# Expert weights of a two-block model read as halves of full rows, in eight rotating slots

## The reference

```python
D_MODEL, SEQ, N_EXPERTS, CAPACITY_FACTOR = 1024, 256, 16, 2
def expert_choice_moe(h, w_router, w_gate, w_up, w_down):
    cap = max(1, CAPACITY_FACTOR * S // N_EXPERTS)          # 32 tokens for each expert
    logits = jnp.einsum('bsd,de->bse', h, w_router).astype(jnp.float32)
    aff = jax.nn.softmax(logits, axis=-1)
    gate, idx = lax.top_k(aff.transpose(0, 2, 1), cap)
    xin = jax.vmap(lambda hb, ib: hb[ib])(h, idx)
    hid = jax.nn.silu(jnp.einsum('becd,edf->becf', xin, w_gate)) * jnp.einsum('becd,edf->becf', xin, w_up)
    y = jnp.einsum('becf,efd->becd', hid, w_down) * gate[..., None].astype(h.dtype)
    return jnp.zeros_like(h).at[bidx, idx].add(y)
...
x = x + einsum(mixed, w_out)                                 # end of the first block's mixer
x = x + expert_choice_moe(rms_norm(x, norm2_w[l]), ...)      # 16 experts
x = second_block(x, ...)                                     # 2 x (FFN, mixer, FFN)
```

## Time and profile before

| | |
|---|---|
| time, median of 3 runs | 1729.85 us (1727.73 to 1731.01) |
| span of the profiled execution, first to last instruction | 1726.3 us |
| time of the profiled execution itself | not listed apart from the three runs; its span lies 3.55 us under their median |
| PE busy | 1606.1 us, 93% of the span |
| DVE, ACT busy | 43%, 38% |
| read from HBM | 398.23 MB |
| mean granted TensorE clock | 0.936 of full speed |

### The profile page before, as it was taken

How to read it: one execution, slowest core, us unless ns; L and a number is a source line. 1 busy time by engine, 2 the same in 40 slices (tenths; PEclk the granted TensorE clock), 3 DMA queues, 4 the chain that set the end, 5 groups by cost and what they waited for, 6 DMA issues and landing times.

```text
span 1726.3 us, 26493 instructions
## 1 busy us (share of the span) xinstructions
PE 1606.1 (93%) x10974; PEld 1299.6 (75%) x10974; DVE 750.1 (43%) x1004; ACT 663.7 (38%) x757; POOL 46.6 (3%) x34
## 2 busy tenths in 40 slices
PE   7996878897888888999999999999999999999998
PEld 7885744443443444499999979999999999889997
DVE  4679531110101101164445765444554447754444
ACT  5564322111111111354345554433634354753343
POOL 0015200000000000000000000000000000000000
PEclk9898979788778878999999999999999999999999
DMA  7522599999999999965555535555465555346552
GB/s 241 178 80 73 198 339 386 387 387 387 387 387 387 387 387 387 369 220 179 185 191 158 163 98 196 193 178 163 152 215 191 174 170 182 115 138 202 193 181 86
DMA packets 249052, 400.12 MB, mean 232 GB/s; under 512 B 4720, under 2 KB 135200, under 8 KB 248864
## 3 DMA queue, kind: packets, MB, share of 16 engines
q1 hardware_dynamic: 247808, 397.74, 66.8%
q10 hardware_dynamic: 1184, 1.57, 0.3%
HBM read 398.23 MB, written 1.06 MB: 231 GB/s over the span
## 4 chain that ended last, share of the span: by engine, by line
PE 65%; SPq 20%; DVE 5%; DMA 4%; issue 3%; ACT 3%; POOL 0%; ACTq 0%; DVEq 0%; POOLq 0%
SPq L430 20%; PE ps L581 12%; PE ps L583 12%; PE ps L582 12%; PE ps L606 6%; PE ps L607 6%; PE ps L608 6%; PE ps L811 4%; DMA ring<-w_in 2%; PE ps L552 2%; PE ps L543 1%; PE ps L800 1%; DMA ring<-w_expert_down 1%; PE ps L844 1%; PE ps L854 1%
## 5 line engine op out<-in xcount | busy, mean ns | idle before, releaser
L1715 DVE TENSOR_TENSOR wl_sb<-raw_sb,wh_sb 128x2048 fp32r<-128x2048 f32 x162 | 370.8, 2292 | 294.1 <-ACT wh_sb L1220 293.8
L581 PE MATMUL ps<-xTh_sb,wh_sb 128*128 128x256 f32 x1696 | 482.2, 284 | 1.0 <-DVE xTl_sb L1410 1.0
L583 PE MATMUL ps<-xTh_sb,wl_sb 128*128 128x256 f32 x1696 | 479.9, 283 | 0.0
L582 PE MATMUL ps<-xTl_sb,wh_sb 128*128 128x256 f32 x1696 | 479.9, 283 | 0.0
L1220 ACT ACTIVATE wh_sb<-raw_sb 128x2048 fp32r<-128x2048 f32 x162 | 309.8, 1915 | 300.0 <-PE ps L583 186.4
L581 PEld LDWEIGHTS ps<-xTh_sb,wh_sb 128*128 128x128 f32 x1696 | 325.3, 192 | 4.5 <-DVE xTl_sb L1410 2.5
L582 PEld LDWEIGHTS ps<-xTl_sb,wh_sb 128*128 128x128 f32 x1696 | 325.4, 192 | 2.2 <-issue 0.7
L583 PEld LDWEIGHTS ps<-xTh_sb,wl_sb 128*128 128x128 f32 x1696 | 325.4, 192 | 0.0
L811 PE MATMUL ps<-ring,work 128*32 128x512 f32 x1280 | 206.0, 791 | 60.8 <-DMA ring<-w_expert_up 38.9
L811 PEld LDWEIGHTS ps<-ring,work 128*32 128x32 f32 x1280 | 45.7, 136 | 182.6 <-issue 153.1
L606 PE MATMUL ps<-wh_sb,hidh_sb 128*128 128x512 f32 x384 | 151.2, 394 | 1.2 <-DVE wl_sb L1715 1.2
(11 more groups left out here) (294 smaller groups left out, 1775.2 us busy)
## 6 DMA issues: line engine op xcount, KB each, us to landing
ring<-w_expert_down SPq DMA_DIRECT2D x32, 2048.0 KB, 19.7
ring<-w_expert_gate SPq DMA_DIRECT2D x24, 2048.0 KB, 19.4
ring<-w_expert_up SPq DMA_DIRECT2D x24, 2048.0 KB, 19.8
raw_sb<-ffn_gate SPq DMA_DIRECT2D x44, 1024.0 KB, 5.4
raw_sb<-ffn_up SPq DMA_DIRECT2D x44, 1024.0 KB, 5.3
raw_sb<-ffn_down SPq DMA_DIRECT2D x44, 1024.0 KB, 4.9
raw_sb<-w_in SPq DMA_DIRECT2D x22, 1024.0 KB, 5.4
ring<-w_in SPq DMA_DIRECT2D x16, 1024.0 KB, 5.6
```

Of the source, the lines that this page charges most:

```text
L581: pe.matmul(to, w_h[:, k, fs], x_h[:, k, :], start=k == 0, stop=False)
L582: pe.matmul(to, w_h[:, k, fs], x_l[:, k, :], start=False, stop=False)
L583: mm = pe.matmul(to, w_l[:, k, fs], x_h[:, k, :], start=False, stop=k == KD - 1)
L1715: dve.tensor_tensor(wl[j], raw[j], wh[j].bitcast(F32), ALU.subtract).then_inc(raw_free[j], 1)
```

## The change

Each matrix is again fetched in two DMAs of 2 MiB, but a half is now 512 of the 1024 rows with all 1024 columns: a run in HBM is one row, 4 KB, and partition p gets four rows. The 96 halves of the 16 experts are one sequence (gate 0, gate 1, up 0, up 1, down 0, down 1, next expert), half q goes to slot q % 8, and SP waits only for half q - 8 to have been used. As a half now holds part of the rows for all columns, a product writes two PSUM banks and needs both halves before either bank is complete: gate in banks 4 and 5, up in 6 and 7, down in 4 and 5 again. The gather of the next expert's tokens moves from the head of an expert to between the fold of gate and the fold of up, into bank 6. The transpose moves to the head of an expert. The silu is one instruction over all features instead of two. The first fetches of the second block, which go over slots 0 and 1, wait for expert 14 to be done; before, they waited for the last products of gate.

```diff
-            def half(row, w, c, to, landed):
-                rows = w.rearrange("e d f -> (e d) f")[bass.ds(row, D), 512 * c:512 * c + 512]
-                sp.dma_start(to, rows.rearrange("(k p) n -> p k n", p=P)).then_inc(landed, 16)
+            def half(i, row, s):
+                rows = (wg, wu, wd)[i // 2].rearrange("e d f -> (e d) f")[bass.ds(row, D), :]
+                lines = rows.rearrange("(k p) n -> p k n", p=P)
+                sp.dma_start(expert_rows(s), lines[:, (i % 2) * Q4:(i % 2 + 1) * Q4, :]).then_inc(ex_in[s], 16)
...
+            def next_half(q, taken, row):
+                sp.wait_ge(sem["half_used"], taken)
+                half(q % 6, row, q % NS)
+            TURN = 4 * 6
+            with sp.Fori(0, (NE * 6 - NS) // TURN) as g:
+                for j in range(TURN):
+                    next_half(NS + j, sp.snap(TURN * g + j + 1), sp.snap(4 * D * g + D * ((NS + j) // 6)))
+            for q in range(NS + (NE * 6 - NS) // TURN * TURN, NE * 6):
+                next_half(q, q - NS + 1, D * (q // 6))
...
+            def product(b, stationary, q, landed):
+                h, w = q % 2, expert_rows(q % NS)
+                pe.wait_ge(ex_in[q % NS], landed)
+                for n in range(2):
+                    for j in range(Q4):
+                        mm = pe.matmul(bank(b + n)[j * CAP:j * CAP + CAP, :], stationary[:, Q4 * h + j, :],
+                                       w[:, j, 512 * n:512 * n + 512], start=h == 0, stop=h == 1, skip_group_check=True)
+                    if h == 1 and n == 0:
+                        mm.then_inc(sem["n0_ps"], 1)
+                mm.then_inc(sem["half_used"], 1)
...
+                product(GATE_PS, xin, q, landed(q))
+                product(GATE_PS, xin, q + 1, landed(q + 1))
+                pe.wait_ge(sem["back_done"], e_th(1, 1))
+                product(UP_PS, xin, q + 2, landed(q + 2))
+                product(UP_PS, xin, q + 3, landed(q + 3))
+                pe.wait_ge(sem["g4_done"], e_th(2, 2))
+                fold_up(g4, GATE_PS, range(KD)).then_inc(sem["fold_ps"], 1)
+                pe.wait_ge(sem["hot_done"], e_th(1, 2))
+                pe.wait_ge(sem["u4_done"], e_th(2, 1))
                 gather()
+                pe.wait_ge(sem["u4_done"], e_th(2, 2))
+                fold_up(u4, GATE_PS + 1, range(Q4)).then_inc(sem["fold_ps"], 1)
+                fold_up(u4, UP_PS + 1, range(Q4, KD)).then_inc(sem["fold_ps"], 1)
+                pe.wait_ge(sem["ehid_done"], e_th(2, 1))
+                product(GATE_PS, hidT, q + 4, landed(q + 4))
+                pe.wait_ge(sem["ehid_done"], e_th(2, 2))
+                product(GATE_PS, hidT, q + 5, landed(q + 5))
+                pe.wait_ge(sem["y4_act"], e_th(1, 1))
+                pe.wait_ge(sem["y4_dve"], e_th(1, 1))
```

More of the change, by code:

```diff
@@ L259, in two_blocks @@
         r_mx, r_nm, r_sum, r_rec = t2(TT), t2(TT), t2(TT), t2(TT)
-        affT, topw, chosen, place, ones_e = [t2(S)[0:NE, :] for _ in range(5)]
+        topw, chosen, place, ones_e = [t2(S)[0:NE, :] for _ in range(4)]
         top8 = t2(8)[0:NE, :]
@@ L450, in _ @@
             sp.wait_ge(sem["w1_lo"], W1)
-            half(0, wu, 0, slot(2), ex_in[2])
+            half(2, 0, 2)
             sp.wait_ge(sem["acc_done"], 1)
-            for i, w, c in REST[1:]:
-                half(0, w, c, slot(i), ex_in[i])
-            first_half(D, True)
+            for i in range(3, 6):
+                half(i, 0, i)
+            for i in range(2):
+                half(i, D, 6 + i)
             sp.wait_ge(sem["tb_rows_done"], 1)
             sp.dma_start(tb_dram.ap(), tb_rows).then_inc(sem["tb_out"], 16)
[L459 to L482, removed]
@@ new lines, in fold_up, with expert, value, landed @@
+            def fold_up(src, b, ks):
+                for i, k in enumerate(ks):
+                    mm = pe.matmul(bank(b)[:, i * CAP:i * CAP + CAP], src[:, k, :], fold, start=True, stop=True)
+                return mm
+            def expert(g, i):
+                def value(per, v):
+                    return pe.snap(per * g + v)
+                def landed(q):
+                    return value(16 * TURN // NS, 16 * (q // NS) + 16)
+                def e_th(per, v):
+                    return value(4 * per, per * i + v)
+                q = 6 * i
+                pe.wait_ge(sem["hote_done"], e_th(1, 1))
+                for t in range(TT):
+                    mm = pe.transpose(bank(UP_PS + 1)[:, t * P:t * P + P], hot_e[:, t, :, :].rearrange("p j c -> p (j c)"), ident)
+                mm.then_inc(sem["back_ps"], 1)
+                pe.wait_ge(sem["xe_ready"], e_th(1, 1))
+                product(GATE_PS, xin, q, landed(q))
[7 more added lines that the diff above has]
+                pe.wait_ge(sem["u4_done"], e_th(2, 1))
+                gather()
+                pe.wait_ge(sem["u4_done"], e_th(2, 2))
[7 more added lines that the diff above has]
+                pe.wait_ge(sem["y4_dve"], e_th(1, 1))
+                for t in range(TT):
+                    for n in range(2):
@@ L856, in expert @@
                     mm.then_inc(sem["stage_done" if t else "half_done"], 1)
+            TURN = 4 * 6
             pe.wait_ge(sem["tb_rows_done"], 1)
-            with pe.Fori(0, NE // 2) as i:
-                expert(i, 0)
-                expert(i, 1)
+            pe.wait_ge(sem["hot_done"], 1)
+            gather()
+            with pe.Fori(0, NE // 4) as g:
+                for i in range(4):
+                    expert(g, i)
             def parts(j, n):
@@ L1957, in _ @@
             pool.memset(ones_e, 1.0).then_inc(sem["masks_zero"], 1)
-            pool.memset(hot[:, :, NE, :], 0.0).then_inc(sem["masks_zero"], 1)
-            pool.wait_ge(sem["used0"], 2 * NE)
+            pool.memset(hot[:, :, NE:NE + 2, :], 0.0).then_inc(sem["masks_zero"], 1)
+            pool.wait_ge(sem["half_used"], 6 * (NE - 1))
             for j in range(3):
                 pool.memset(hold[:, 1 + j:2 + j], 0.0).then_inc(raw_free[j], 1)
+            pool.wait_ge(sem["half_used"], 6 * (NE - 1) + 3)
+            for j in range(3):
+                pool.memset(hold[:, 6 + j:7 + j], 0.0).then_inc(used[j], 1)
             pool.wait_ge(sem["stage_done"], NE)
```

153 lines of the change are left out of this document (54 added, 99 removed).

## The result

The changed kernel takes 1709.92 us (median of 4 runs, 1707.82 to 1712.10) against 1730.43 us before (4 runs, 1727.73 to 1731.70): a ratio of 0.989 with an interval of 0.987 to 0.991. The forecast was 1708.8 us, 1.1 us less. The four runs fall into two pairs: 1707.8 and 1707.9 at a mean granted clock of 0.937 and 0.936, 1712.0 and 1712.1 at 0.925. The profiled execution is one of the slower pair (1711.96 us, 2.0 above the median). A run's time is about 1.8 us longer than its span, so the profiled execution of before, with a span of 1726.3, took about 1728.1 us, 2.3 under the median. So the two traces differ by 16.1 us where the medians differ by 20.5.

What follows compares the result with a forecast made beforehand. The prediction took the expert fetch stream at 387 GB/s to bound the first block. Stream -26.1, ahead +1, behind +4 gave -21.1 us, from 1729.85 to 1708.8 us; range from one below 1700 up to 1720.

Steps and rivals of the forecast that it cites:

- The rate of the stream: Expert fetches: 4 KB runs raise the long stream from 387 to 409 GB/s, so 88 halves take 26.1 us less.
- The line of 37.7 ns for a kilobyte and 9 ns for a run: Expert fetches: time per run from the rates at 1 and 2 KB, giving 160.1 ns or 409 GB/s at 4 KB.
- The 4.2 us kept for the slow start and the last landing: Stream's two ends: time left over when 88 halves are summed from SP's first reissue, kept the same before and after.
- Ahead of the stream: Before SP's first reissue: DVE's `hot_e` products and two transposes now come first, moving it to about 243.7; +1 us (0 to 2).
- Behind the stream: Last landing to end of last scatter: new fetch order leaves more PE work there; +4 us, 2.2 at full clock, +18 at low.
- The 0.7 us for DVE's multiply: After the last expert's fold of up: DVE's multiply with its wait, counted as 0.7 us ahead of down.
- The two signs that the forecast named for this place: End of the last expert: last scatter 8 to 14 us behind the last landing, and near 708 us.
- The cover: Inside the experts: PE keeps pace with the stream, 29.7 us an expert against a new period of 30.7, holding by 1.0 us.
- rival B: Inside the experts: PE becomes the bound, at a mean clock of about 0.79 instead of 0.82; 1722 us, chance 0.11.
- Edits at nothing: `xin` wait gone, `y4` wait added, one silu, SP's issues, second block's first fetches: all hidden or unchanged, no time.
- The sum: Whole kernel: -26.1 + 1 + 4 = -21.1 us, taking the median from 1729.85 to 1708.8 us.
- its bounds 401 GB/s and +9 us: Forecast's own limits: stream rate 401 to 413 GB/s, end +2 to +9 us, given as 1703 to 1718 us; chance 0.74.

Runs made afterwards that it cites:

- e1: The changed kernel with each half fetched as two 1 MiB DMAs cut by columns, so runs are 2 KB again; 1737.78 us, ratio 1.0040 to the kernel before.
- e2: The changed kernel with each half fetched as two 1 MiB DMAs cut by rows, so runs stay 4 KB; 1709.49 us, ratio 0.9873 to the kernel before.
- e4: The changed kernel fetching only half the rows, products using them twice, so PE's work is the same but output is wrong; 1683.65 us, ratio 0.9715.
- e3: The changed kernel with 16 KB runs, PE's left operands of gather and fold read with a step of four elements; 1759.09 us, ratio 1.0163.
- e6: The changed kernel with the scatter waiting for each copy of `y4` only where it reads it; 1712.08 us, ratio 0.9894.
- e10: The changed kernel with the gather moved between down's products and the scatter, and the last expert's gather left out; 1708.74 us, ratio 0.9874.
- e8: The changed kernel with 16 KB runs, feature order set in ACT's and DVE's copies so PE's left operands stay contiguous; 1688.95 us, ratio 0.9763.
- e5: The changed kernel without the last expert's gather, which picks tokens for an expert that doesn't exist; 1708.77 us, ratio 0.9877.
- e11: The changed kernel with 16 KB runs ordered in copies, the gather behind down and no last gather; 1688.30 us, ratio 0.9758.

## Why the prediction was right

**The rate of the stream.** Forecast: 409 GB/s, -26.1 us. The changed kernel shows 409 to 410, the last landing is 25.4 us earlier (forecast -26.1 + 1 = -25.1), and e1 and e2, which differ by the run alone, are 28.3 us apart. The line of 37.7 ns for a kilobyte and 9 ns for a run was laid through the rates at 1 and 2 KB (349 and 387 GB/s); it foretold 409 at 4 KB, which was measured, and gives 428 at 16 KB, where 430 to 432 were. The 4.2 us kept for the slow start and the last landing were right too: 244.14 + 450.8 + 4.2 = 699.1 against 698.4. The Trainium skill ("DMA: Bandwidth & Descriptors", Specifications) gives 512 B as the minimum transfer for line rate. By that, 2 and 4 KB would be alike; e1 and e2 show 387 and 409 GB/s, and the measurement decides.

**Ahead of the stream.** +1 us, measured 0.94.

**Behind the stream.** This is the step that was mis-sized: +4 us forecast, +9.3 in the profiled execution (15.0 us from the last landing to the end of the scatter, forecast 9.7). Counted from the landing, the product of up 1 ends at -5.3 and not at -8.4, because PE was still working off gate when up 1 had landed: +3.1. Gather 4.52 instead of 3.65, fold 3.60 instead of 1.9, down 6.16 instead of 3.6: +5.1, from a clock at 0.51. The 0.7 us for DVE's multiply did not appear. Together 7.5 us, where 15.0 is 7.1 above the 7.9 of the forecast's own count. The forecast took a nearly full clock and an idle PE here, and gave as its reason that the mean of the whole stretch was 0.82. But e4, at a mean of 0.81, has its low clock in just these steps, from the gather to down, and so have early experts of the changed kernel (gather 4.49, fold of up 3.60, down 6.19 us in the second). The trace of before could not show this for the new order, but it had its own sign: down took 5.25 us in the last expert, and not 3.64. The two signs that the forecast named for this place, a last scatter 8 to 14 us behind the last landing and near 708 us, failed as well (15.0, 713.42). The profiled execution of e1 has 16.3 us there (725.5; 741.83). The faster pair of runs took 4.1 us less on the whole; whether that lies at the end is not shown, as neither of them was traced. The medians of e1 and before put both costs together, ahead and behind, at 6.8 us, where the forecast has 5.

**The cover.** Forecast 29.7 us of PE against 30.7. Measured by the same sum: 412.15 x 30.7 / 437 = 29.0 busy, and 0.9 for `y4`, 29.9. It held by 0.8 us, which are the 11.1 us of waits that remain; the forecast had named at least 1 us an expert. The clock fell to 0.78, under the 0.79 at which rival B would begin, and B still did not come. So the margin is not as thin as the sum makes it: a PE that isn't held up needs 27.5 us (e4), 3.2 under the period. With e3's strided loads B came true.

**Edits at nothing.** The wait for `xin` before each expert is gone and that for `y4` is there, 14.7 us in all; e6 takes it away and e10 hides it, and neither is faster. The second block has its old length, and SP's queue has 1% of the chain.

**The sum.** By the traces -25.4 + 9.3 = -16.1 us, the difference of the two spans. By the medians -20.5, forecast -21.1. The mechanism is the forecast one, but that the number came within 1.1 us is in part luck: in the profiled execution the end cost 5.3 us more than forecast, and two of the four runs were 4 us shorter than that one. By the medians of e1 and e2 the gain is 28.3 us and the costs 6.8, each 2 us above the forecast; the intervals of these ratios are 2.5 to 2.9 us to either side, so neither difference is clear of noise. Two sums of the prediction are off without effect on it: its bounds 401 GB/s and +9 us taken together give 1723 us and not 1718, and 408.7 GB/s gives -25.3 us and not -25.5.

## What to carry to other kernels

Where windows show a flat rate with the DMA share at 1, look at the contiguous run before the number of queues or buffers: two run lengths in one trace give a line (time for a kilobyte, time for a run), and here it foretold two others. A layout that lengthens the run is worth having if the change of order can be put into a copy that is made anyway, not into a left operand of PE. What stands behind the last landing is to be priced by the durations of the same steps in an earlier pass, not by the mean clock, and one traced execution stands for the others only as far as its time and granted clock agree with theirs.

## What the runs showed of the hardware that was not expected

- The rate of one core's stream from HBM depends on the run up to 16 KB: 349 GB/s at 1 KB, 387 at 2 KB, 409 at 4 KB, 430 at 16 KB. At 4 KB it is the same with two DMAs of 1 MiB a half as with one of 2 MiB.
- A left operand read with a step of four fp32 elements slows PE's weight loads: half a fold (16 instructions) takes 3.94 us at full clock and 3.92 at the low one, where one with a contiguous operand takes 1.97 and 3.60 (e3, changed kernel). Copies of 128x512 fp32 out of PSUM that read with such a step take 597 ns on ACT and 692 on DVE (e8), where those without it take 598 and 692.
- The granted clock falls to 0.50 in a PE that has no idle time: in e4 it is 0.81 over 402 us with PE busy for 97%, and low from the gather on in each expert. In e6 and e10 it is low after a wait for a fetch as well, while in e5 a wait of the same 3.10 us leaves the fold behind it near full speed. What decides it in a given expert is not settled by these runs. With the gather behind down (e10 and e11) the mean over the execution is 0.949 to 0.951 in six of the seven runs that count, and no run is faster for it.
